# Attention of a two-block transformer kernel: scores and minimum moved ahead of the transposes and the copy

## The reference

```python
# phase A: window attention, 8 query heads on 2 key heads, a sink column
s_loc = einsum('bnqkgd,bnjkd->bnkgqj', qb, kb) * scale;  s_loc = where(mask, s_loc, -inf)
s_ctx = einsum('bnqkgd,bjkd->bnkgqj', qb, k_ctx) * scale
p = softmax(concatenate([s_loc, s_ctx, sink_col], -1)); o = p_loc @ vb + p_ctx @ v_ctx
# phase B: neighbourhood attention on a 16 x 64 grid, 8 heads, a relative bias, no sink
s_loc = einsum('bnqhd,bnjhd->bnhqj', qb, kg) * scale + bias;  s_loc = where(mask, s_loc, -inf)
p = softmax(concatenate([s_loc, s_ctx], -1)); o = p_loc @ vg + p_ctx @ v_ctx
```

## Time and profile before

| | |
|---|---|
| median of 3 runs | 2825.46 us |
| profiled execution, its span | 2823.26 us, 2821.4 us |
| TensorE busy over the span | 2628.9 us (93%) |
| VectorE busy | 1246.9 us (44%) |
| ScalarE busy | 782.7 us (28%) |
| GpSimd busy | 415.5 us (15%) |
| phase A of the attention | 394 to about 546 us |
| tables and first rounds of phase B | about 546 to 562 us |
| rest of phase B | 562 to 757 us |

### The profile page before, as it was taken

The page is one execution under the profiler, slowest core; times in us unless marked ns, Lnnn a source line. Parts: engine busy times, 40 slices in busy tenths (PEclk is TensorE's granted clock), DMA queues, the critical chain, the costliest instruction groups (busy, mean ns, idle before and its releaser), DMA issues. The chain is left out here.

```text
span 2821.4 us, 42122 instructions
## 1 busy us (share of the span) xinstructions
PE 2628.9 (93%) x16281; PEld 2264.0 (80%) x16281; DVE 1246.9 (44%) x1918; ACT 782.7 (28%) x1472; POOL 415.5 (15%) x522
## 2 busy tenths in 40 slices
PE   5799979898798999999999999998889999999998
PEld 2788967787697888888888799976877888888887
DVE  3533257767556233333333432027254444454456
ACT  2422245555613111111111232234242111211122
POOL 2474212222103000000000100005030000000001
PEclk8899989999899999999999999998989999999999
DMA  7233310000130111111111121110311111111111
GB/s 273 90 120 119 104 37 1 1 2 0 61 120 30 46 45 47 59 45 45 46 59 45 67 96 38 46 27 1 120 38 45 48 56 45 45 59 45 45 45 75
DMA packets 118855, 164.58 MB, mean 58 GB/s; under 512 B 5448, under 2 KB 103692, under 8 KB 118412
## 3 DMA queue, kind: packets, MB, share of 16 engines
q1 hardware_dynamic: 118732, 162.87, 17.4%
HBM read 154.45 MB, written 9.41 MB: 58 GB/s over the span
## 5 line engine op out<-in xcount | busy, mean ns | idle before, releaser
L387 PE MATMUL ps<-w_hi,ht_hi 128*128 128x256 f32 x1808 | 521.3, 288 | 18.9 <-DVE w_lo L373 9.8
L388 PE MATMUL ps<-w_lo,ht_hi 128*128 128x256 f32 x1808 | 515.3, 285 | 0.0
L389 PE MATMUL ps<-w_hi,ht_lo 128*128 128x256 f32 x1808 | 514.9, 285 | 0.0
L1395 DVE TENSOR_TENSOR q_nat<-q_nat,ps 128x512 f32<-128x512 f32 x384 | 261.2, 687 | 549.9 <-PE ps L1379 549.9
L1355 PE MATMUL ps<-ht_hi,w_hi 128*128 128x512 f32 x1216 | 476.8, 392 | 6.5 <-DVE w_lo L373 3.8
L1356 PE MATMUL ps<-ht_lo,w_hi 128*128 128x512 f32 x1216 | 476.2, 392 | 0.0
L1357 PE MATMUL ps<-ht_hi,w_lo 128*128 128x512 f32 x1216 | 475.8, 391 | 0.0
L369 ACT ACTIVATE w_hi<-stage 128x2048 fp32r<-128x2048 f32 x97 | 185.5, 1913 | 780.4 <-PE ps L1379 464.9
L387 PEld LDWEIGHTS ps<-w_hi,ht_hi 128*128 128x128 f32 x1808 | 349.3, 193 | 35.6 <-DVE w_lo L373 11.5
L373 DVE TENSOR_TENSOR w_lo<-stage,w_hi 128x2048 fp32r<-128x2048 f32 x97 | 224.9, 2319 | 297.2 <-ACT w_hi L369 297.1
L388 PEld LDWEIGHTS ps<-w_lo,ht_hi 128*128 128x128 f32 x1808 | 349.5, 193 | 0.0
(11 more groups left out here) (239 smaller groups left out, 3076.3 us busy)
## 6 DMA issues: line engine op xcount, KB each, us to landing
stage<-w_ff SPq DMA_DIRECT2D x32, 1024.0 KB, 5.2
stage<-w_in SPq DMA_DIRECT2D x24, 1024.0 KB, 5.2
stage<-w_mod SPq DMA_DIRECT2D x16, 1024.0 KB, 5.4
stage<-w_gate SPq DMA_DIRECT2D x11, 1024.0 KB, 5.2
stage<-w_up SPq DMA_DIRECT2D x11, 1024.0 KB, 5.1
stage<-w_down SPq DMA_DIRECT2D x11, 1024.0 KB, 4.9
mod_w<-w_mod SPq DMA_DIRECT2D x8, 1024.0 KB, 12.6
q_nat<-x SPq DMA_DIRECT2D x16, 512.0 KB, 10.0
```

What stands on the lines that cost most here:

```text
L387: pe.matmul(bank, a, wh[:, k, :], start=(k == 0), stop=False)
L388: pe.matmul(bank, a, wl[:, k, :], start=False, stop=False)
L389: mm = pe.matmul(bank, b, wh[:, k, :], start=False, stop=(k == KT - 1))
L1395: dve.tensor_tensor(row, row, ps[:, 4 + o % 4, :], ALU.add).then_inc(evac, 1)
```

## The change

On TensorE the scores of the next unit are issued ahead of transposing this unit's probabilities, for each head. They no longer wait for the previous exp, where that exp reads only `masked`: there they wait for the previous minimum. On VectorE the minimum of the next unit stands ahead of the copy of this unit's transposed probabilities, for each head. The minimum has a wait of its own for the exp whose input it overwrites. The order of the values, the queries and the output, all of ScalarE, GpSimd and SyncE stay.

```diff
+        def scores_read(ph, i, n):
+            where = ph if n or not isinstance(i, int) or i else A
+            return min_done if joined(where, (n - 1) % NB) else exp_done
...
-                    pe.wait_ge(exp_done, 2 * u - 1 + j)
+                    pe.wait_ge(scores_read(ph, i, n), 2 * u - 1 + j)
...
                         ahead, behind = not (last and n + 1 >= NB), not (first and n == 0)
-                        pe_turn_p(pe, ph, i, n, 0)
                         if ahead:
                             pe_scores(pe, ph, *after(i, n, 1), 0)
+                        pe_turn_p(pe, ph, i, n, 0)
                         if behind:
                             pe_values(pe, ph, *before(i, n))
                         if not (last and n + 2 >= NB):
                             pe_turn_q(pe, ph, *after(i, n, 2))
-                        pe_turn_p(pe, ph, i, n, 1)
                         if ahead:
                             pe_scores(pe, ph, *after(i, n, 1), 1)
+                        pe_turn_p(pe, ph, i, n, 1)
                         if behind:
                             pe_turn_o(pe, ph, *before(i, n))
...
             if ph == A and n == 0:
                 dve.drain()
+            if not isinstance(u, int) or u > 0:
+                dve.wait_ge(exp_done, 2 * u - 1 + j)
+            if ph == A and n == 0:
                 dve.wait_ge(s_done, 2 * u + j + 1)
...
-                        dve_p(dve, ph, i, n, 0)
                         if ahead:
                             dve_min(dve, ph, *after(i, n, 1), 0)
+                        dve_p(dve, ph, i, n, 0)
                         if behind:
                             dve_o(dve, ph, *before(i, n))
-                        dve_p(dve, ph, i, n, 1)
                         if ahead:
                             dve_min(dve, ph, *after(i, n, 1), 1)
+                        dve_p(dve, ph, i, n, 1)
                         dve_sums(dve, ph, i, n)
```

## The result

The kernel after the change took 2835.72 us (median of six runs, 2831.11 to 2843.15) against 2825.28 for the kernel before in the same job (2820.99 to 2826.77). The ratio is 1.004, 95% interval 1.0026 to 1.0055: slower, by some 10 us, outside the predicted 2813 to 2831. The profiled execution took 2835.05 us, its span 2833.2.

What follows compares the result with a forecast made beforehand. TensorE's own instructions, busy 90% in attention phase A, set most of the time. Steady rounds +7.3, A pair ends -1.6, B pair ends -8.4, clock +1.2, starts -1.9, tails -0.9 sum to -4.3 us: median 2821.2, range 2813 to 2831.

Steps and rivals of the forecast that it cites:

- the chain M1, P1, T0: Second head's next minimum, then VectorE copy of its transposed probabilities, then next head-0 transposes: TensorE idle 0.76 (A), 0.44 (B).
- rival (c): Single bank and VectorE's order decide: steady rounds lose over about 0.3 us, exp wait adds 0.08; 2832 us, chance 0.15.
- signs of being wrong: No wait before head-0 transposes in steady rounds, as many clock falls as before, or idle ahead of scores, counted at nothing.
- +0.17: Each steady round of phase A gets 0.17 us longer, 4.63 in all; counted for 20 rounds.
- +0.23: Steady rounds of phase B get 0.23 us longer each (wide ones 0.25); counted for 17 rounds.
- the stop of 0.25 goes: Steady round of A: idle 0.25 us before the values disappears, as the output multiply comes at 2.2, before their turn at 2.5.
- Rival (a): Steady-round stops are smaller than worked out, the copy starting less late: +7.3 us shrinks to 2; time 2816, chance 0.26.
- 0.05 either way: Rounds between the steady ones and the ends, whose next scores are narrow, change by 0.05 us either way.
- the pair ends of A: Values wait less for `v_pair`: 0.44 us shorter, the round before gains 0.1; three ends, -1.6 us.
- I take six tenths of three falls at 0.7: Phase B, longer idle before round 7's second-head transposes, behind the tables, may drop TensorE's clock: +1.2 us.
- rival (b): Clock still falls at B's three pair ends, losing 3 x 1.4 us: 2825.4; chance 0.17 together with the rival of no effect.
- The starts: Starts of phases A and B get shorter, by 1.5 and 0.4 us, as both minima move up: -1.9 us.

Runs made afterwards that it cites:

- run 1: Changed kernel with VectorE's order undone (copies ahead of the minima again), TensorE's new order and new waits kept: 2851.28 us, ratio 1.0104 to the kernel before.
- run 2: Changed kernel with the wait for the mask and bias tables only ahead of the first minimum: 2832.37 us, ratio 1.0037 to the kernel before.
- run 5: Kernel before, with the queries' transposes put ahead of the values on TensorE: 2813.28 us, ratio 0.9965.
- run 4: Kernel before, with the copy making `v_pair` issued on ScalarE ahead of the second exp of round 1: 2803.47 us, ratio 0.993.
- 9: Changed kernel with `v_pair` copied ahead of the second exp of round 1: 2826.72 us, ratio 1.0013 to the kernel before.

## Why the prediction was wrong

What bounds the kernel, that only the attention moves, and the chain M1, P1, T0 behind the single bank were right (run 1 takes the copy out from behind the minimum, and the stop before T0 halves). The end was that of rival (c), in a direction to which the prediction gave 0.12: slower, since a steady round lost over 0.3. (Its own sum gives 2833.5, not the 2832 that it names.) Its price for the added wait was not seen: the trace names the scores, and not the exp, as what M1 waited for, and another wait taken away changed no round (run 2). Two of the signs of being wrong that the prediction names came as well: the clock's falls at the pair ends were as many as before, and S0 stood idle, which was counted at nothing (0.45 at the end of a pair shown above, 0.18 and 0.24 at two ends of A). Three terms of the sum failed, the first of them by 7.9 us of the 14.4 between forecast and measurement.

**The steady round, mis-sized: +0.17 was +0.47 (written out) and +0.38 (looped) in A; +0.23 was 0.47 and 0.37 in B.** The step that failed is "the stop of 0.25 goes". I took the idle time ahead of V as a wait for the output multiply, which should be met by then. It was met, but 0.17 of the stop is a changeover (run 5), which stays in every order run here. My own sum of the pair end had counted a gap of 0.17 behind V as work, while the same gap ahead of V was counted as a wait. By the prediction V comes 0.50 behind T0; in the round above it comes 0.70 behind (426.71 to 427.41). In the looped rounds these 0.20 are nearly the whole miss: 4.84 for 4.63, and most of it in B, 5.96 for 5.84.

The written-out rounds have 0.11 more: M1 starts 0.47 behind T1 and not 0.36, since its scores start 0.52 ahead of T1 and not 0.54, and M1 0.99 behind them and not 0.90. This 0.90 was misread. In the kernel before, the row of VectorE ahead of the minimum at 425.61 is

```profile
424.91 0.69 DVE L958 COPY prob_t<-ps 128x512 f32<-128x512 f32 x1 [0.72 <-PE ps L780]
```

The copy ends at 425.60, so that minimum started when VectorE was free, and the row does not tell how soon it can follow its scores. The 0.20 and the 0.11 make the 4.93, within 0.01. Rival (a), which held the idle 0.76 for too much, was wrong: it is 0.82 written out and 0.73 looped.

**Rounds with narrow scores, "0.05 either way", and with them the pair ends of A.** The last rounds of a pair grew like the steady ones: 4.14 to 4.46 and 4.54 to 4.85 at the first end (from O to O). The wait for `v_pair` did shrink, 1.92 to 1.02, and its round from 6.03 to 5.59, the predicted 0.44. The two rounds ahead of it gave 0.63 back at the first end and 0.38 at the others. Three ends gave +0.1 instead of -1.6.

**The clock at the pair ends of B.** "I take six tenths of three falls at 0.7" was the wrong size. The two halves of the forecast held: behind the wait for `v_pair`, cut to 0.78 and 1.16, there is no fall, and behind the tables, where 2.65 idle came for the predicted 2.7, there is. But it came three times of three (twice in run 2, which has the same order), and at a place where it costs more than 0.7: S0 and T0 take 1.35 and 0.80 in place of 0.78 and 0.42, about 0.95 on the path, beside 0.45 of wait. With them the first round takes 6.67 for 5.23. So the falls moved and did not become fewer, which is what rival (b) had priced for the other place. In the kernel before, the idle 2.19 there was followed by none; in run 4, with the same 2.19, there was one each time, so the length of the stop alone does not decide it. That the wait for M1 and the exp made `v_pair` late was right: runs 4 and 9 put `v_pair` ahead of that exp, and the wait of the values all but goes.

The starts gave 1.1 of the predicted 1.9, the tails 0.4 of 0.9. Of the 1.5 at the start of A 0.9 is the wait of the values (1.99 to 1.08). The rest goes with the clock, which fell there in the kernel before (398.9) and not after; no run shows that the change did this.

The Trainium skill (TensorE: Matmul & The Clock Gate, Part 4: PE-mode transpose), which the prediction weighed, holds that transposes do not count as TensorE being busy in the same way. For it there is now a row: from the end of the scores at 670.5 to V at 673.1 TensorE did nothing but transposes, 0.6 us of them, in 2.6 us, as long as the idle 2.55 that a fall followed before. The clock stayed at 1.00, at all three ends. This does not settle the rule, since wholly idle stops of that length did not always bring a fall either (2.75 us ahead of V at 563.86 in the kernel before, with the clock at 1.00 behind it), and no run took the transposes alone away. The rounds that the prediction calls half transposes have about two fifths of their busy time in them.

## What to carry to other kernels

When a stop in front of an instruction is to be removed, look first whether the same idle time stands where no wait can be (behind that instruction, in other rounds): that part belongs to the instruction and stays. A row gives the delay from one instruction to the next only if the second one was waiting for it: look at what else its engine did until then. The steady round here has several chains that end nearly together (T0 for the copy, V for the output, S0 for the queries, all within 0.4 us), so cutting one moved the stop to the next, and an order that lengthened one of them cost that much in every round. The wait that comes once in eight rounds was cheaper to mend where it arises, by moving one call on ScalarE, than by reordering the rounds.

## What the runs showed of the hardware

Ahead of and behind weight tiles of 64 columns, between tiles of 128, TensorE's loads stand still for 0.17 us (0.17 to 0.20 ahead of them in B), in nearly every round of the kernels run here; with the clock down it is 0.33.

The clock's fall has no sharp edge in the idle time shown. In run 5 TensorE stood idle 3.13 ahead of T1 of round 7 at two ends of B, at the same place of the program (weight loads):

```profile
645.80 0.42 PEld L780 LDWEIGHTS ps<-ident,probs 128*128 128x128 f32 x4 [3.13 <-issue]
...
646.41 0.78 PEld L770 LDWEIGHTS ps<-kt,q_t 128*128 128x128 f32 x6
...
694.41 0.42 PEld L780 LDWEIGHTS ps<-ident,probs 128*128 128x128 f32 x4 [3.13 <-issue]
...
695.01 1.24 PEld L770 LDWEIGHTS ps<-kt,q_t 128*128 128x128 f32 x6
```

The first time the loads kept their full speed, the second time they did not. So it was with V of run 1 in A after 2.43 idle: once 0.85 for its 16 loads, once 1.39 for the 14 that the trace has.

Rounds written out take 0.09 more than the same rounds in a loop, in the changed order only; neither the third wait nor the reset explains it, and it stays open.
